# An input projection in three fp32r passes, split piece by piece, and 15 gathered row products moved from the gate table to the experts

## The reference

```python
h = rmsnorm(x, norm1_g[l])
proj = h @ w_in[l]
qa, ka, va, qb, kb, vb, ga, gb = jnp.split(proj, IN_SPLIT_POINTS, axis=-1)
ya = neighbourhood_attention(qa, ka, va, na_rpb[l])        # shapes left out
qh = axial_rope(rmsnorm(qb, gqa_q_norm_g[l]))
kh = axial_rope(rmsnorm(kb, gqa_k_norm_g[l]))
yb = gqa_attention(qh, kh, vb)
merged = jax.nn.sigmoid(ga) * (ya @ w_proj_a[l]) + jax.nn.sigmoid(gb) * (yb @ w_proj_b[l])
x = x + merged @ w_out[l]
x = x + peer(rmsnorm(x, norm2_g[l]), peer_w_q[l], peer_sub_keys[l], peer_u[l], peer_v[l])
```

## Time and profile before

| what | us |
|---|---|
| median of three runs | 2494.54 |
| the profiled execution | 2491.89 |
| its span | 2490.1 |
| PE busy (share of the span) | 2318.8 (93%) |
| PE weight loads (PEld) | 1781.3 (72%) |
| DVE busy | 1418.5 (57%) |
| ACT busy | 754.0 (30%) |
| POOL busy | 434.6 (17%) |
| products of the projection, first to last | 20.4 to 144.2 |
| first product of attend | 157.07 |
| table, PE's first early product to its last | 604.3 to 1037.3 |
| experts, PE's first product to its last | 1048.7 to 1873.5 |

### The profile page before, as it was taken

How to read it: one execution, slowest core, us unless ns; L and a number is a source line. 1 busy time by engine, 2 the same in 40 slices (tenths; PEclk the granted TensorE clock), 3 DMA queues, 4 the chain that set the end, 5 groups by cost and what they waited for, 6 DMA issues and landing times. The chain is left out here.

```text
span 2490.1 us, 27351 instructions
## 1 busy us (share of the span) xinstructions
PE 2318.8 (93%) x10409; PEld 1781.3 (72%) x10409; DVE 1418.5 (57%) x2554; ACT 754.0 (30%) x1310; POOL 434.6 (17%) x306
## 2 busy tenths in 40 slices
PE   7989899899995989899999999999994999989889
PEld 4457666687553757688889999999984898865444
DVE  1325423335989998567775677777776624424331
ACT  1124412221111628533333333333333322211110
POOL 1100000000224010012221445444451000013100
PEclk9999899999998999999999999999997899989899
DMA  4230133201787565889996879888873222120110
GB/s 183 101 98 26 55 115 124 96 34 49 241 276 258 154 231 172 286 276 338 337 329 242 278 268 317 292 291 288 293 259 140 86 101 96 57 110 35 51 68 34
DMA packets 203859, 440.97 MB, mean 177 GB/s; under 512 B 13392, under 2 KB 126544, under 8 KB 196944
## 3 DMA queue, kind: packets, MB, share of 16 engines
q1 hardware_dynamic: 166864, 304.98, 36.0%
q0 software_dynamic: 36864, 134.23, 15.5%
HBM read 399.45 MB, written 39.71 MB: 176 GB/s over the span
## 5 line engine op out<-in xcount | busy, mean ns | idle before, releaser
L1387 PE MATMUL bank<-Vh,Hh 128*128 128x512 f32 x768 | 299.5, 390 | 3.2 <-DVE Hl L1471 3.2
L1389 PE MATMUL bank<-Vh,Hl 128*128 128x512 f32 x768 | 300.6, 391 | 0.0
L1388 PE MATMUL bank<-Vl,Hh 128*128 128x512 f32 x768 | 300.6, 391 | 0.0
L803 POOL DMA_INDIRECT ring<-in_v,gidx x128 | 221.6, 1731 | 235.8 <-DVE x_res L815 109.9
L1414 ACT ACTIVATE Vh<-Vr 128x1024 fp32r<-128x1024 f32 x128 | 135.7, 1060 | 304.4 <-PE bank L1389 304.4
L768 PE MATMUL bank<-XT,ur 128*128 128x384 f32 x624 | 213.6, 492 | 4.5 <-DMA ur<-in_u 4.5
L1370 PE MATMUL bank<-Xh,Uh 128*128 128x384 f32 x560 | 188.7, 337 | 11.4 <-DVE Xl L1476 11.4
L1466 DVE TENSOR_TENSOR Vl<-Vr,Vh 128x1024 fp32r<-128x1024 f32 x128 | 156.4, 1222 | 70.7 <-ACT Vh L1414 68.8
L1449 DVE TENSOR_TENSOR Ul<-ur,Uh 128x1024 fp32r<-128x1024 f32 x70 | 85.7, 1224 | 185.1 <-ACT Uh L1399 185.1
L1372 PE MATMUL bank<-Xh,Ul 128*128 128x384 f32 x560 | 188.5, 337 | 0.0
L1371 PE MATMUL bank<-Xl,Uh 128*128 128x384 f32 x560 | 188.2, 336 | 0.0
(11 more groups left out here) (316 smaller groups left out, 4420.9 us busy)
## 6 DMA issues: line engine op xcount, KB each, us to landing
Vr<-in_v SPq DMA_DIRECT2D x128, 512.0 KB, 5.7
ur<-in_u SPq DMA_DIRECT2D x109, 512.0 KB
W<-in_w_stream SPq DMA_DIRECT2D x26, 2048.0 KB, 7.9
gates<-stage SPq DMA_DIRECT2D x48, 512.0 KB, 6.0
Gr<-gates SPq DMA_DIRECT2D x64, 384.0 KB
w_raw<-in_w_mixer SPq DMA_DIRECT2D x14, 1024.0 KB, 4.8
XT<-in_w_mixer SPq DMA_DIRECT2D x12, 1024.0 KB
early<-ar SPq DMA_DIRECT2D x58, 192.0 KB
```

The source lines that it names most:

```text
L803: pool.indirect_dma_start(out=self.ring[s % RG], out_offset=None, in_=table, in_offset=at).then_inc(self.landed[s % RG], 16)
L1387: pe.matmul(ps, Hh[r][:, tok], Vh[r][:, cut], start=p == 0, stop=False)
L1388: pe.matmul(ps, Hh[r][:, tok], Vl[r][:, cut], start=False, stop=False)
L1389: mm = pe.matmul(ps, Hl[r][:, tok], Vh[r][:, cut], start=False, stop=p == PK - 1)
```

## The change

Three things change, and one follows.

1. The projection is computed as three fp32r products per product, in 36 pieces of 512 weight columns (eight pieces for a 512-wide block, four for B_KVB). ACT rounds each piece (`hi`), DVE takes the rest (`lo`), in three buffers each. x is split as well: ACT writes `Xh` from the turned bank, DVE writes `XT` and `Xl`. The order of the last two blocks is now B_KA, B_QA. The groups of a block alternate between banks 4 to 7 and banks 0 to 3.
2. The turns of the nine heads stand inside B_QA, behind its second piece (`TURN`), and the store of va stands on SP behind the third block, not behind the fifth.
3. `DOTS_TAIL` is (0, 13, 0, 3) where it was (0, 13, 13, 5), so 43 row products are done in the table phase and 85 in the experts, where it was 58 and 70.
4. Buffers move: QK and S1 lie in the space of kT and qzb (`kq`), HN in that of y, `qpad` in that of qz, which POOL clears twice.

```diff
-DOTS_LINK, DOTS_TAIL = 9, (0, 13, 13, 5)
+DOTS_LINK, DOTS_TAIL = 9, (0, 13, 0, 3)
...
-B_QB, B_KVB, B_VA, B_QA, B_KA = range(5)
+B_QB, B_KVB, B_VA, B_KA, B_QA = range(5)
...
+IN_PIECE = 512
+IN_PIECES = [(b, part) for b in range(5) for part in range(4 if b == B_KVB else 8)]
...
             for b in range(5):
                 sp.wait_ge(grp, 4 * (b + 1))
                 c.load_w(sp, b + RING)
-            sp.wait_ge(grp_a, 12 - SHARED // 2)
-            sp.dma_start(t["va"].rearrange("(t p) d -> p t d", p=P), a.va[:]).then_inc(va_kept, 16)
+                if b == B_VA:
+                    sp.wait_ge(grp_a, 12 - SHARED // 2)
+                    sp.dma_start(t["va"].rearrange("(t p) d -> p t d", p=P), a.va[:]).then_inc(va_kept, 16)
...
+            def hi(i):
+                c.wait_w(act, IN_PIECES[i][0])
+                if i - 3 in ends:
+                    act.wait_ge(grp, 4 * (ends[i - 3] + 1))
+                elif i >= 3:
+                    act.wait_ge(pieced, i - 2 - IN_PIECES[i - 3][0])
+                act.activation(Wh[i % 3][:], piece(i), ACT.Copy).then_inc(c.whi, 1)
...
+            for i in range(3):
+                hi(i)
             act.wait_ge(c.const_in, CONST_FIRST)
-            gains_act(act, c, C_G1, T_FIRST)
+            for k in range(KT):
+                act.wait_ge(c.turned, T_FIRST * KT + k + 1)
+                act.activation(Xh[:, k], c.bank[k % 4][:], ACT.Copy, scale=c.cols[:, C_G1 + k:C_G1 + k + 1]).then_inc(c.xhi, 1)
+            for i in range(3, N):
+                hi(i)
+                if i - 3 in ends:
+                    out(ends[i - 3])
...
+            for k in range(KT):
+                gain, turned = c.cols[:, C_G1 + k:C_G1 + k + 1], c.bank[k % 4]
+                dve.wait_ge(c.xhi, S_PROJECT + k + 1)
+                dve.tensor_scalar(c.XT[:, k], turned[:], gain, None, ALU.mult).then_inc(c.out_d if k % 2 else c.out_a, 1)
+                dve.scalar_tensor_tensor(out=Xl[:, k], in0=turned[:], scalar=gain, in1=Xh[:, k].bitcast(F32),
+                                         op0=ALU.mult, op1=ALU.subtract).then_inc(c.xlo, 1)
+                if k < 3:
+                    lo(k)
...
+            for k in range(KT):
+                if k >= 4:
+                    pe.wait_ge(c.out_d if k % 2 else c.out_a, k // 2 - 1)
+                    pe.wait_ge(c.xlo, S_PROJECT + k - 3)
...
+            def products(i):
+                b, part = IN_PIECES[i]
+                width = 256 if b == B_KVB else 512
+                ks = IN_PIECE // width
+                pe.wait_ge(c.wlo, i + 1)
+                if b == 0:
+                    pe.wait_ge(c.xlo, S_PROJECT + ks * (part + 1))
+                if part == 0 and b == 1:
+                    transposed_pe(pe, c, T_FIRST)
+                for n in range(4):
+                    g = 4 * b + n
+                    if part == 0:
+                        if 4 + SHARED <= g:
+                            pe.wait_ge(grp_a, g - 3 - SHARED // 2)
+                        elif g >= 8:
+                            pe.wait_ge(grp_d if g % 2 else grp_a, (g - 8) // 2 + 1)
+                    for k2 in range(ks):
+                        k = part * ks + k2
+                        first, last = k == 0, k == KT - 1
...
+                            pe.matmul(ps, xh, wh, start=first, stop=False)
+                            pe.matmul(ps, xh, wl, start=False, stop=False)
+                            mm = pe.matmul(ps, Xl[:, k, n * P:(n + 1) * P], wh, start=False, stop=last)
...
+            for i in range(N):
+                products(i)
+                if i == TURN:
+                    pe.wait_ge(roped, 1)
+                    pe.wait_ge(grp_a, 12)
+                    for h in range(HEADS + 1):
```

More of the change, by code:

```diff
@@ L315, in _, with out @@
         def _(act):
+            copy = lambda o, i, s: act.activation(o, i, ACT.Copy, scale=s)
+            def hi(i):
[5 more added lines that the diff above has]
+                act.activation(Wh[i % 3][:], piece(i), ACT.Copy).then_inc(c.whi, 1)
+            def out(b):
+                for g in range(4 * b, 4 * b + 4, 2 if b in (B_QB, B_KVB, B_QA) else 1):
+                    act.wait_ge(grp, g + 1)
+                    if g == 12:
+                        act.wait_ge(roped, 1)
+                    if g == 16:
+                        act.wait_ge(set0, 4)
+                    project_out(g, copy, grp_a)
             for tt in range(TT):
@@ L351, in _ @@
             dve.wait_ge(c.const_in, CONST_FIRST)
-            gains_dve(dve, c, C_G1, T_FIRST)
-            for g in range(1, SHARED, 2):
-                dve.wait_ge(grp, g + 1)
-                project_out(g, lambda o, i, s: dve.tensor_scalar(o, i, s, None, ALU.mult), grp_d)
-            link = lambda ins: c.link(dve, ins)
+            for k in range(KT):
[6 more added lines that the diff above has]
+                    lo(k)
@@ L359, in _ @@
+            for i in range(3, 11):
+                lo(i)
+            out(B_QB)
+            for i in range(11, 14):
+                lo(i)
+            out(B_KVB)
+            lo(14)
             dve.wait_ge(grp_a, SHARED // 2)
             dve.wait_ge(grp_d, SHARED // 2)
-            flat = lambda x: x[:].rearrange("p t w -> p (t w)")
-            heads = lambda x: x[:].rearrange("p t (h w) -> p (t h) w", w=DH)
+            flat = lambda x: x.rearrange("p t w -> p (t w)")
+            heads = lambda x: x.rearrange("p t (h w) -> p t h w", w=DH)
@@ L363, in _ @@
+            rooted = lambda x: x.rearrange("p (t h) -> p t h", t=TT)
             link(dve.tensor_tensor(flat(S1), flat(QK), flat(QK), ALU.mult))
-            dve.tensor_reduce(hs[:, 0], heads(S1), AX, ALU.add).then_inc(hsum, 1)
+            lo(15)
+            dve.tensor_reduce(rooted(hs[:, 0]), heads(S1), AX, ALU.add).then_inc(hsum, 1)
+            for i in range(16, 20):
+                lo(i)
             dve.wait_ge(hroot, 1)
-            link(dve.tensor_tensor(heads(S1), heads(QK), bc(hs[:, 2], DH), ALU.mult))
@@ L385, in _ @@
                 last = dve.tensor_tensor(KR[:, tt], S1[:, tt, ATT_W:], S2[:, tt, ATT_W:], ALU.add)
+                if tt == 1:
+                    lo(27)
             last.then_inc(roped, 1)
+            for i in range(28, TURN + 4):
+                lo(i)
             for h in range(1, HEADS, 2):
@@ L389, in _ @@
                 dve.tensor_scalar(a.qzb[:, h], c.bank[h % 4][:], DH ** -0.5, None, ALU.mult).then_inc(rout_d, 1)
+            for i in range(TURN + 4, N):
+                lo(i)
+            out(B_QA)
         @block.tensor
@@ new lines, in _ @@
+            for i in range(N):
[4 more added lines that the diff above has]
+                    for h in range(HEADS + 1):
+                        if h >= 4:
+                            pe.wait_ge(rout_d if h % 2 else rout, h // 2 - 1)
+                        for tt in range(TT):
+                            src = qpad[:, tt, h] if h < HEADS else KR[:, tt]
+                            mm = pe.transpose(c.bank[h % 4][:, tt * P:(tt + 1) * P], src, c.ident)
+                        mm.then_inc(rturn, 1)
```

132 lines of the change are left out of this document (74 added, 58 removed).

## The result

The changed kernel takes 2449.82 us (median of four runs, 2448.57 to 2451.39) against 2494.53 us (2493.21 to 2496.31, four runs). The ratio is 0.9821, with a 95% interval of 0.9804 to 0.9838: faster by 1.8%. The forecast was 2449.7 us. The medians lie 44.7 us apart. The profiled execution took 2448.57 us, 43.3 less than that of before (2491.89); its span is 2446.8 us, also 43.3 less.

The account below looks back on a forecast made before the run. PE was taken as the bound: full in projection and experts, waiting for va's store and DVE's hot rows. Projection -23.6, table -22.5 and experts +1.3 sum to -44.8 us, so 2449.7 us against the median, range 2441 to 2461.

Parts of the forecast that it names:

- Products, -25.3: Projection: 480 fp32r products take 98.5 us where the products before took 123.8, so 25.3 us less.
- Start, +5.2: Start of the projection: splitting x and weights delays the first product from 20.4 to 25.6, 5.2 us more.
- Clock at the start, +1.5: Start of the projection: PE, nearly idle between the turns, begins at a low clock, 1.5 us more.
- Two gaps, +2.7: First groups of B_KA and B_QA: PE stands for one `hi` and one bank copy each, 2.7 us more.
- End, -6.8 and -0.9: Projection's end: without the wait for va's store attend starts 6.8 us sooner; the clock staying up gains about 0.9.
- Splitting beside the products, 0: Projection: two pieces, 5.4 us, cover the 4.1 us splitting chain, and `roped` comes near 100, so PE does not wait.
- Table, -20.1 and -2.4: Table phase: row products leave PE's gaps before slices(0) and slices(1), 20.1 and 2.4 us less.
- Experts, +1.3: End of the experts: the last three iterations hold eight additions instead of seven, 1.3 us more.
- I cost them at nothing: Experts: fifteen more row products, 18.3 us of DVE, are covered by PE's products and cost nothing.
- DMA share and GB/s: Rival, experts short of DMA: four more rows there cost 6.3 us, gain 38.5 us, 2456; chance 0.07.
- the 18.3 us of the row products: Rival, DVE short of time in the experts: the 18.3 us return, gain 26.5 us, 2468; chance 0.04.
- the clock did not fall in the projection: Rival, slower: stops at the pieces make the 480 products run at 1.2 GHz, 87 us more, 2537; chance 0.02.

Follow-up runs that it names:

- The run with the other order: The changed kernel with PE's turns, ACT's roundings and DVE's operations reordered at the start of the projection, same instructions: ratio 0.9794 to the kernel before, span 2441.1 us.
- the run without them: The changed kernel with B_KA's groups waiting only for the pieces and B_QA's for the copy eight groups before: ratio 0.9812 to the kernel before, span 2445.9 us.
- the row products alone: The kernel before with only DOTS_TAIL changed, to (0, 13, 0, 3): ratio 0.9925, span 2470.1 us.
- the projection alone: The changed kernel with DOTS_TAIL put back to (0, 13, 13, 5): ratio 0.9901 to the kernel before, span 2467.5 us.

## Why the prediction was right

The mechanisms held: fewer PE cycles in the projection, the store's wait gone, DVE's row products taken out of PE's gap. The profiled executions lie 43.3 us apart where the sum said 44.8. That the median met the forecast to 0.1 us is luck: the sum was 1.5 us too large, and the profiled execution, from which it was counted, lay 2.65 us below its median before and 1.25 now. Several small misses also cancel. One sum was off: the bounds of the terms, added up, reach from about -57 to -28 us and not from -52 to -37. Step by step:

- **Products, -25.3.** The spacing is 0.227 us for 512 columns (88 distances between 29.63 and 49.62 take 19.99 us) and 0.120 for 256. All 480 come to 98.9 us, block by block and without the low clock at the start and the gaps, against the 98.5 of the sum, so 24.9 us less. The rule of the Trainium skill (TensorE: Matmul & The Clock Gate, Back-to-back issue gap), N/2.4 + 2.5 ns for a product without its weight load, gives 93.4 as an estimate (the prediction has 93.3). The trace lies 5.5 us above it, with a weight load for every product; whether the loads are the difference no run here shows. For a stream of products with their loads the same section of the Trainium skill states about 131 ns at 512 columns; the 227 ns here disagree.
- **Start, +5.2.** Measured +5.8 (26.23 for 20.41). From DVE's first `XT` (18.19) to the first product it takes 8.0 us, and the sum had 8.0 (17.6 to 25.6). What came 0.6 us late is the start of the chain: x and the first weight block landed later, and ACT rounded the first piece at 15.84, not 15.3. PE's first turn stands at 14.0 to 15.0 in every run with the new projection and at 13.7 in the three with the old one; why was not tried. The run with the other order shows that the chain is what the products waited for.
- **Clock at the start, +1.5.** Measured 1.6.
- **Two gaps, +2.7.** Two of 1.36 us; 2.8 us by the run without them.
- **End, -6.8 and -0.9.** Attend starts 1.8 us behind PE's last product, for 2.0. The store explains it in both directions (+10.8 us at attend when put back, -7.6 when moved alone). The clock's part, 0.9, measured 0.8 in the changed kernel, against the run with the store last, and 2.2 in the old one; the whole stretch behind attend's first product is 1.6 us shorter than before.
- **Splitting beside the products, 0.** PE waits for `lo` nowhere. `roped` is signalled near 102, for 100, and PE asks for it at 113.37.
- **Table, -20.1 and -2.4.** Measured -19.4 for the first. For the second the gap shrank by 2.45, but slices(1) came only 1.1 earlier. The slices did start at the low clock, but not "as before": the first 16 products and the four behind them took 5.8 us now (768.06 to 773.86), and 4.6 before (810.27 to 814.90), although the gap ahead of them was the longer one then. That is no work of the change: with the row products alone they took 4.6 us behind a gap of 7.45, and there slices(1) came 2.3 us earlier, as forecast; with the projection alone they took 5.9 behind 28.62.
- **Experts, +1.3.** Measured +1.3 up to acc, but the number is right partly by luck: the tail, all that the term held, grew by 0.7, and the other 0.65 lies ahead of PE's last product. "I cost them at nothing" was nearly right: PE's waits for `Hl` grew from 3.2 to 4.2 us, and to 5.2 with the row products alone.
- **Not forecast, -1.5:** PE's gap ahead of the experts is 9.84 us; in the trace of before it was 11.41. It is 9.5 to 10.4 in every run with the new projection and 11.2 in the two without it. What links them was not tried.

The rivals: DMA share and GB/s rose from 0.86 and 294 to 0.88 and 303 in the experts, and PE waited 1.0 us more there, for DVE; of the 18.3 us of the row products 1.3 came back; and the clock did not fall in the projection. There the prediction's picture was off: PE hardly stops between the pieces. Apart from the two gaps of 1.36 us its products start 0.227 us apart across them. The Trainium skill on cycling through banks (TensorE: Matmul & The Clock Gate, A second HAM failure mode: psum-queue depth-cycling) speaks of short pauses between groups. With two such pauses and a granted clock of 1.00 the projection neither bears it out nor speaks against it, and nor does the merge's window, in which PE is busy for 100.00 of 100 us.

## What to carry to other kernels

A product's own time is read from the distance of two starts in a phase that already uses the form, weight loads included; 480 of them were then right to 0.4 us. Before costing a shorter phase, look at what its end waits for: here a store issued last kept PE standing for 8.8 us, of which 0.9 stayed without it and no faster product would have touched the rest, and its place is worth 9.6 to 13.0 of the projection's 22.6 us. Work moved to a covered phase is paid for at that phase's end, so deal it out to be done a little early.

## What the hardware showed that I had not expected

- **The clock falls while PE is full.** In or just behind a row of products of 16 columns, 0.11 us apart and without a gap, the granted clock goes to 1.2 GHz, with 96 of them for 13.5 to 20.5 us and with 24 for some 3. The Trainium skill (TensorE: Matmul & The Clock Gate, Why this matters for your kernels) ties a fall in mid-kernel to gaps in which PE is idle; here there was none.
- **A longer pause did not bring a longer ramp.** After 27.85 us without work the first twenty products of slices(0) took 4.6 us, after 28.62 us 5.9, after 8.41 us 5.8, after 7.45 us 4.6.
- **Going from turns straight into products costs hardly a ramp.** With the first product 7.8 us earlier, right behind four turns that PE did without a wait (turns from 15.01, product at 18.40), one product ran at the low clock instead of eight.
